# Prompt attention of a hybrid encoder step: one run of values products per head pair, and a next-pair score split around a transpose group

## The reference

```
def block(args):
    qb, pb = args
    s = jnp.einsum('bqhd,bkhd->bhqk', qb, k, preferred_element_type=F32) * scale
    mask = k_chunk[None, :] <= (pb // CHUNK)[:, None]
    p = jax.nn.softmax(jnp.where(mask[None, None], s, -jnp.inf), axis=-1)
    return jnp.einsum('bqhk,bkhd->bqhd' ...
```

## Time and profile before

| what | value |
|---|---|
| time, median of 3 runs | 4063.73 us (4062.64 to 4065.74) |
| the profiled execution | 4062.5 us, of which the span from first to last instruction is 4060.7 us |
| PE busy | 3856.2 us, 95% of the span |
| DVE, ACT, POOL busy | 1750.6 us (43%), 1329.3 us (33%), 162.8 us (4%) |
| granted PE clock, mean | 0.98 of full speed |
| prompt attention | about 1622 to 2281 us of the span |

### The profile page before, as it was taken

One profiled execution on the slowest core, in us unless ns is written; L12 is line 12 of the kernel. 1 busy time (PEld: TensorE's weight loads), 2 busy tenths in 40 slices (PEclk: granted clock), 3 DMA queues, 4 the chain that ended last, 5 costly groups with the idle time before them and its releaser, 6 DMA issues. The chain is left out here.

```text
span 4060.7 us, 58877 instructions
## 1 busy us (share of the span) xinstructions
PE 3856.2 (95%) x22777; PEld 2747.9 (68%) x22777; DVE 1750.6 (43%) x4462; ACT 1329.3 (33%) x3419; POOL 162.8 (4%) x186
## 2 busy tenths in 40 slices
PE   8899999988999897899999899899999999899999
PEld 1677777767999754566666444667777677577776
DVE  0343344344555423565555322222112221399996
ACT  0111111115555322665555200122211221155553
POOL 1000000010010000000000000000000000001010
PEclk9899999999999999999999999999999999899999
DMA  9211111132310002100000344211111111343433
GB/s 358 66 52 58 44 44 51 56 66 68 92 57 32 29 15 56 32 26 16 16 13 9 123 174 145 94 67 62 57 67 72 67 62 58 133 160 127 165 124 112
DMA packets 117020, 317.18 MB, mean 78 GB/s; under 512 B 38552, under 2 KB 54712, under 8 KB 110584
## 3 DMA queue, kind: packets, MB, share of 16 engines
q1 hardware_dynamic: 113928, 287.79, 19.9%
q0 software_dynamic: 2928, 27.16, 2.0%
HBM read 205.16 MB, written 109.74 MB: 78 GB/s over the span
## 5 line engine op out<-in xcount | busy, mean ns | idle before, releaser
L2230 PE MATMUL e_p<-e_hT,w_ahead 128*128 128x128 f32 x3264 | 410.3, 276 | 4.1 <-DMA shared<-w_in_o 4.1
L2230 PEld LDWEIGHTS e_p<-e_hT,w_ahead 128*128 128x128 f32 x3264 | 388.9, 193 | 12.1 <-issue 12.1
L500 PE MATMUL a_p<-w_even,a_hT 128*128 128x512 f32 (+2 forms) x1088 | 391.9, 521 | 0.0
L485 PEld LDWEIGHTS a_p<-a_hT,w_even 128*128 128x128 f32 x3264 | 369.6, 193 | 15.5 <-issue 15.5
L485 PE MATMUL a_p<-a_hT,w_even 128*128 128x128 f32 x3264 | 369.8, 276 | 7.5 <-DVE a_hT L301 7.5
L500 PEld LDWEIGHTS a_p<-w_even,a_hT 128*128 128x128 f32 x1088 | 205.3, 190 | 174.1 <-issue 122.2
L1616 DVE TENSOR_REDUCE q_mx<-q_sps 128x1 f32<-128x512 f32 (+4 forms) x320 | 181.5, 583 | 215.7 <-PE q_sps L1457 214.8
L2096 PE MATMUL c_b<-shared,c_oc 128*128 128x512 f32 x544 | 239.7, 600 | 20.6 <-DMA c_xt<-x_prompt 13.7
L2601 PE MATMUL h_b<-h_w,h_oT 128*128 128x512 f32 x544 | 250.4, 595 | 0.0
L2188 ACT ACTIVATE e_r<-e_p 128x512 f32<-128x512 f32 x68 | 40.6, 598 | 523.4 <-PE e_p L2236 303.9
L2096 PEld LDWEIGHTS c_b<-shared,c_oc 128*128 128x128 f32 x544 | 103.3, 192 | 156.4 <-issue 136.7
(11 more groups left out here) (414 smaller groups left out, 6237.7 us busy)
## 6 DMA issues: line engine op xcount, KB each, us to landing
scr_qkg<-e_r SPq DMA_DIRECT2D x68, 512.0 KB, 2.6
h_rq<-scr_qkg SPq DMA_DIRECT2D x17, 2048.0 KB, 10.8
wa<-w_ada SPq DMA_DIRECT2D x16, 1536.0 KB, 12.8
scr_iz<-e_r SPq DMA_DIRECT2D x34, 512.0 KB, 2.7
scr_qkv<-a_cv SPq DMA_DIRECT2D x17, 768.0 KB, 3.3
d_sc<-scr_qkv SPq DMA_DIRECT2D x17, 768.0 KB, 4.3
w_even<-w_in_e POOLq DMA_DIRECT2D x8, 1620.0 KB, 35.3
w_ahead<-w_in_o POOLq DMA_DIRECT2D x6, 2048.0 KB, 9.0
```

Source lines behind the costliest of these rows:

```text
L485: mm = pe.matmul(bank[g][:, (c % 4) * P:(c % 4 + 1) * P], w[:, k, c * P:(c + 1) * P], hT[:, p, k, :], start=k == 0, stop=k == KD - 1)
L500: mm = pe.matmul(dst[:, 0:b - a], hT[:, p, k, :], w[:, k, a:b], start=k == 0, stop=k == KD - 1)
L2230: mm = pe.matmul(bank[n % 4][:, c * P:(c + 1) * P], w[k][:, a:a + P], hT[:, p, k, :], start=k == 0, stop=k == KD - 1)
```

## The change

The products of a pair are taken out from between the transposes and put in one run at the pair's end. With four groups the second head's scores of the next pair are cut in two halves: the first two banks stand behind group 1, the last two behind group 2. With three groups they stay behind group 1, whole. So that all groups of a pair can wait for their products, `q_PT` gets four slots in place of two. The lists of DVE and ACT keep their order; only the slot number in `turn` changes.

```
-        PT = sb(f"{tag}_PT", [P, 2, 2, 512])
+        PT = sb(f"{tag}_PT", [P, SLOTS, 2, 512])
...
-            def scores(z, h):
+            def scores(z, h, half=None):
...
-                for b in range(z.nb):
+                first = -(-z.nb // 2)
+                for b in (range(z.nb), range(first), range(first, z.nb))[0 if half is None else half + 1]:
...
                 for b in range(z.ng):
                     transposes(z, j, b, 0)
                     transposes(z, j, b, 1)
-                    if b:
-                        products(z, j, b - 1)
-                    if b == z.mid and nz:
+                    if nz and z.ng == 4 and b in (1, 2):
+                        scores(nz, 2 * nj + 1, b - 1)
+                    elif nz and z.ng < 4 and b == z.mid:
                         scores(nz, 2 * nj + 1)
-                products(z, j, z.ng - 1)
+                for b in range(z.ng):
+                    products(z, j, b)
```

More of the change, by code:

```diff
@@ L1291, in attention @@
     PAIRS = HB // 2
+    SLOTS = 4
     with ExitStack() as ctx:
@@ L1481, in products @@
                     pe.wait_ge(oU_r, z.p0 + j)
-                n = z.turned(j, b) % 2
+                n = z.turned(j, b) % SLOTS
                 for i in range(4 * b, min(4 * b + 4, z.kt)):
@@ L1558, in turn @@
                 w = min(4, z.kt - 4 * b) * P
-                act.copy(PT[:, z.turned(j, b) % 2, 0, 0:w], tps[0][:, 0:w]).then_inc(pt_a, 1)
+                act.copy(PT[:, z.turned(j, b) % SLOTS, 0, 0:w], tps[0][:, 0:w]).then_inc(pt_a, 1)
             def pair(z, j):
@@ L1625, in turn @@
                 w = min(4, z.kt - 4 * b) * P
-                dve.tensor_copy(PT[:, z.turned(j, b) % 2, 1, 0:w], tps[1][:, 0:w]).then_inc(pt_b, 1)
+                dve.tensor_copy(PT[:, z.turned(j, b) % SLOTS, 1, 0:w], tps[1][:, 0:w]).then_inc(pt_b, 1)
             def gates(z):
```

## The result

| kernel | median | runs |
|---|---|---|
| before | 4063.73 us | 11 runs, 4057.21 to 4069.00 |
| after | 4075.78 us | 11 runs, 4067.49 to 4080.78 |

The ratio is 1.0025, with a 95% interval of 1.0016 to 1.0035: 10 us slower by the ratio, 6.5 to 14.2 by its interval, 12 by the medians. The predicted 4070.4 us was 5.4 us too low, inside its range. The line between no change and slower lay at 4071.9 us; the median is above it, and the interval holds it.

A forecast was written before the change was run, and what follows sets the result against it. PE, busy almost without a gap, was taken to bound the kernel. 26.1 + 0.4 - 9.5 - 5.4 - 5.9 + 1.0 = +6.7 us on 4063.7 gave 4070.4 us, range 4064 to 4079 us.

The forecast's parts named there:

- The line between no change and slower: For the whole program, 0.2% (8.1 us) that a measurement can tell from no change, up to 4071.9 us.
- Three groups, -10.3 us: 16 pairs with three groups: -5.4 us for a products run removed, -5.9 for a wait gone, +1.0 for late scores.
- The +1.0 us: Seven three-group pairs whose next scores have three banks: the third bank waits for ACT and shows a weight load, 0.15 us each.
- The new wait: Group 3's second-head transposes wait for DVE's copy of group 2 in 15 four-group pairs, 1.65 to 1.87 us each, +26.1 us.
- The runs that go away, -9.5 us: Two separate products runs no longer entered and left in 15 four-group pairs, 0.63 us a pair.
- the last pair, +0.4 us: The stage's last pair, without next scores: two more waits for copies, 0.5 to 1.4 us, less 0.6 for two runs.
- rival 3: Scores cut behind transposes show weight loads of 0.10 us, 46 times, 4.6 us: 4075 us, slower; chance 0.06.
- rival 1: DVE's copy comes before group 3's second half is due, so 26.1 us fall out: 4044.3 us, faster; chance 0.06.
- The clock stays at 1.00: Expected sign in the changed profile: PE's granted clock does not fall in this stage.
- its own last sentence: Wrong if group 3 doesn't wait, three groups aren't some 10 us shorter, four not some 17 longer, or the clock falls.
- Rival 2: Each of 15 new waits at group 3 brings 6.83 us at half speed, 51 us in all: 4121 us, slower; chance 0.06.

The follow-up runs named there:

- e2: After, but with the second head's scores left whole behind group 1 in pairs with four groups too; 4055.2 us, ratio 0.9989 to before.
- e3: The change in pairs with three groups alone, those with four keeping before's order; 4054.11 us, ratio 0.9977 to before.
- e5: After, but with four groups the products of group 0 stand ahead of group 3's transposes again; 4055.31 us, ratio 0.9977 to before.
- e1: After, with DVE's second-head maxima also cut in halves around the copy of group 2 in pairs with four groups; 4045.32 us, ratio 0.9955 to before.
- e4: The change in pairs with four groups alone, those with three keeping before's order; 4088.46 us, ratio 1.0062 to before.
- e6: The kernel after, unchanged, measured and profiled again on a second chip; 4076.5 us, ratio 1.0036 to before.
- e7: After, with one more DVE maximum of 512 columns ahead of the copy of group 2; 4089.28 us, ratio 1.0060 to before.
- e8: e1 with first-head scores and maxima also cut, three-group second-head ones too, group 0's products behind group 1; 4048.88 us, ratio 0.9964 to before.

## Why the prediction was right, and where it fell short

- **Three groups, -10.3 us:** measured -10.90, and -10.84 to -10.89 in e2, e3 and e5. The wait ahead of the last group's products is gone: nothing is left of the 0.30 us of the earlier trace rows. The +1.0 us is there too: in a pair of after whose next scores have 12 key tiles the second head's take 1988.07 - 1985.33 = 2.74 us, the first head's 1982.80 - 1980.23 = 2.57, and the 0.17 us between them are about the 0.15 forecast.
- **The new wait:** right in its place, its count and its size. It comes 15 times, from DVE's copy of group 2, and from group 3's first to its second half pass 1.93 us, the chain that I had taken from between groups 0 and 1 of the kernel before. Against e1 the fifteen waits cost 26.5 us, where the prediction has 26.1. Without the falls the stretch would be 25.4 - 5 x 1.66 = 17.1 us longer, against 26.1 - 9.5 + 0.4 = 17.0. (1.66 us is the price of one fall, 4.87 - 3.21, from the same 56 instructions in after and e1.)
- **The runs that go away, -9.5 us, and the last pair, +0.4 us:** e1, where the fifteen waits are gone, measures both together: -9.4 us. The last pair, from group 0's transposes to the end of its products, takes 2279.66 - 2271.13 = 8.53 us before and 2262.69 - 2253.71 = 8.98 in e1, 0.45 us more. That leaves -9.9 us for the runs.
- **The cut is free** (against rival 3): eight transposes up to the scores still take 2108.89 - 2108.02 = 0.87 us, as in the earlier trace rows. And rival 1, no wait, is what e1 makes true: it stands for 19.4 us less than before, and e1 was measured at 17 us less.
- **The step that failed is "The clock stays at 1.00".** In the two profiled executions of after it falls at three and at five of 15 pairs, which is 5.0 and 8.3 us. That is the size of the 5.4 us by which the median is above the prediction, but how often the clock fell in the run at the median no profile shows, and runs of before differ by as much. By its own last sentence the prediction is wrong here: the clock falls, and the four groups take 25 us more and not 17. Rival 2 had the mechanism and not the size: it priced 15 falls of 6.83 us, 51 us in all. The row that I held against it, an idle of 1.70 us that left the clock at 1.00, came from a stage where PE was busy for 7.37 of 10 us; a wait of that length in a stage where PE otherwise hardly stands still is another case, and I had no row of that. Why the clock held there and not here, no run shows.
- **The range held by some luck.** It went up to 4079 us to hold rival 3, which did not come; the falls took the room that was left for it. Two readings beside it are off: the middle of the range 4066 to 4077 us is 4071.5, so the line of 4071.9 lies 0.4 us above the middle and 1.5 above the forecast; and from group 3's start to the first products pass 2112.49 - 2110.19 = 2.30 us with 14 key tiles, not 2.5, since group 3 has fewer transposes there than group 0.

What is shown is that the falls come and go with the wait: there are three to seven in after, e4, e6 and e7, with fifteen waits of 1.4 to 2.3 us, and none in before, e1, e2, e3, e5 and e8, where PE waits in this stretch for 0.6 us at most. Why they stand at it with 13 and 14 key tiles and not with 15 and 16, and why the same kernel has three in one execution and five in another, stays open.

## What to carry to other kernels

When a step is moved in one engine's list, look at each engine that answers it and ask which result stands in that engine's list behind something that the move has made later: here PE's scores moved back and DVE's copy, ready but listed behind their maxima, went back with them. Here the two lists had to move together to gain with four groups; the same order of PE was 12 us slower than before with DVE's old list and 17 us faster with DVE's cut at the same place. And a new wait in a dense stretch of PE is to be priced with some falls of the clock on top, as a part of the waits and not as none or all (here three to seven at 15 waits, 1.66 us for one that PE works through).

## What was not expected of the hardware

A wait of 1.55 us in the middle of a stretch in which PE hardly stood still was followed, 0.40 us after its end (2112.12 to 2112.52), by 3.41 us at a granted clock of 0.50, that is 1.2 in place of 2.4 GHz, and then by 1.00 again, with PE busy all through the fall. Waits of up to 0.6 us at the same point of the list (e2, e5) had no such sequel, and neither had waits of 2.0 to 2.1 us with 15 and 16 key tiles (e7).
